# Block-diagonal gates of a recurrent head group as 64-row products on the two halves of the array

## The chip, the cores and the metric

The kernel runs on one core of one Trainium2 chip. The metric is the device time of one execution in microseconds (us), as the median of several runs. The engines are named as in the profile: PE is TensorE (PEld are its weight loads), DVE is VectorE, ACT is ScalarE, POOL is GpSimd, and SP is the engine that issues the DMAs.

## The reference

One layer of a hybrid trunk, on a prompt of 2048 positions of width 1024 and on 8 short sequences of 4 positions (the decode part). A pre-norm and a modulation give hn; one projection gives six groups of 512 columns; group A (RG-LRU) and group B (HGRN2) run side by side; one output projection, a post-norm and a gated residual follow. What the change touches are the two gates r and i of group A, whose weights are eight diagonal blocks of 64 x 64 each:

```python
def _rglru(x, h0, wa, ba, wx, bx, lam):
    B, L, _ = x.shape
    xb = x.reshape(B, L, N_BLK_A, BLK_A)
    r = jax.nn.sigmoid(jnp.einsum('blnc,ncd->blnd', xb, wa).reshape(B, L, D_A) + ba)
    i = jax.nn.sigmoid(jnp.einsum('blnc,ncd->blnd', xb, wx).reshape(B, L, D_A) + bx)
    log_a = -C_RGLRU * jax.nn.softplus(-lam.astype(jnp.float32)) * r.astype(jnp.float32)
    a = jnp.exp(log_a)
    u = jnp.sqrt(jnp.maximum(-jnp.expm1(2.0 * log_a), 0.0)) * (i * x).astype(jnp.float32)
    u = u.at[:, 0].add(a[:, 0] * h0.astype(jnp.float32))
    _, h = lax.associative_scan(_lin_comb, (a, u), axis=1)
    return h, h[:, -1]
```

## The kernel before

The prompt is worked through in 8 bodies of 256 positions (body 0, a loop over bodies 1 to 6, body 7); the decode part is the tail behind body 7. Each engine has its own program, written out by hand in one order, and semaphores tie them together. `Signal.at(n, j)` is the count that a semaphore has reached after j steps of body n. An engine that waits holds up everything behind it on its queue.

Within a body the four blocks of 128 channels of group A, and the four heads of group B, are taken in two halves, p = 0 and p = 1. TensorE's order in a body is: projections of the forget gate and q for p = 0 (`project`, L390, three products of 16-bit halves for each fp32 one); between them `turn_y` of the body before (L441); row projections of v and the gate path with the levels of group B (`level`, L462, L464, L469) in between; the output rows of the body before (`out_rows`, L390); `turn_k` (L477) and the two units (`unit`, L491 to L493); then the same for p = 1, with xa and ga of group A. The first gates, `gates(n, 0)`, stand behind level 3 of p = 1, ahead of the second half of a projection. The second gates, `gates(n, 1)`, stand behind `turn_k(n, 1)` and six products of `out_rows`, ahead of the two units that end the body. The next body begins with a wait for `i_sig` (the sigmoids of i), then `project` twice (48 products), then `turn_y`, which waits for `yb_ok` (the scaled rows that VectorE writes, L1195) and writes the banks aux.

`gates` (L507) makes four fp32 products of 128 x 128 weights with 256 columns: two blocks for r into one bank of aux, two for i into the other, each tied to its own semaphore (gr_ps, gi_ps). Half of every weight tile in `wg` is zero, since the blocks are 64 wide; POOL zeroes it at the start. Levels 1 to 5 use 64 columns of q; level 6 (L469) uses column tiles of 32, level 7 of 64. In the tail, `d_states` (L757) has products of 32 rows, and the decode gates (L794) are eight products with 32 columns.

ScalarE's order around the first gates is `ga_out`, `gates_out` (two sigmoids for r, L903, two for i, L908, each 128 x 256 with a bias per partition), `xa_out` (L879), `decay`, `root`. Around the second gates it is `k_out` (the copy that kt_sb counts, L865), `squares_m` (L861), `gates_out`, `squares_o` of one unit (L872), `squares_m`, `squares_o` of the other unit, `decay`, `root`. VectorE's `rows` waits for the last squares, takes a reciprocal root in twelve small steps and scales four blocks (L1195). POOL's `gated` multiplies i by the convolved input.

At the start SP issues the loads of the conditioning, two early weight pieces, ten rows of parameters (L307, into `am`, turned by TensorE into `par`, from which `pcol` takes the biases), and then the weight pieces in order, with `wg` behind piece 6.

Of the kernel before, what the change touches and what calls it, by code (L numbers as in the profile page):

```python
# [38 lines left out]
ACT = mybir.ActivationFunctionType  # L39
# [28 lines left out]
_at = 0  # L68
for _name, _n in (("pre", KT), ("post", KT), ("cw", CW * CT), ("cb", CT), ("ba", CT), ("bx", CT), ("lam", CT),
                  ("lbl", CT), ("onw", CT), ("adab", 3 * KT)):  # L70
    ROW[_name] = _at
    _at += _n
# [3 lines left out]
def build(nc, x_prompt, x_sample, state_rglru_h, state_rglru_conv, state_hgrn_S, c_prompt, c_sample, ada_w, ada_b,  # L76
          pre_norm_w, post_norm_w, w_in, conv_w, conv_b, rg_wa, rg_ba, rg_wx, rg_bx, rg_lambda, hg_lb_logits,
          hg_onorm_w, w_out, y_prompt, y_sample, h_prompt, conv_prompt, S_prompt, h_sample, conv_sample, S_sample):
    with ExitStack() as ctx:
# [33 lines left out]
        sil = sb("sil", [P, CT, T])  # L113
        wg = sb("wg", [P, 2, CT, P])

# [57 lines left out]
        u_ps = Signal("u_ps", 4)  # L173
        gr_ps, gi_ps = Signal("gr_ps", 2), Signal("gi_ps", 2)

# [4 lines left out]
        xa_sb, ga_sil = Signal("xa_sb", 2), Signal("ga_sil", 2)  # L180
        r_sig, i_sig, a_exp, th_ok = (Signal(s, 4) for s in ("r_sig", "i_sig", "a_exp", "th_ok"))
        u_sqrt = Signal("u_sqrt", 2)
# [109 lines left out]
        def _(sp):  # L292
# [12 lines left out]
            for name, src in loads:  # L305
                rows = src.rearrange("(r c) -> r c", c=P)
                sp.dma_start(am[ROW[name]:ROW[name] + rows.shape[0], 0, :], rows).then_inc(par_ld, 16)  # L307
            for i, (kind, c) in enumerate(pieces):
                if i == 3:
                    for t in range(NT):  # L310
                        sp.dma_start(xin[:, t, :], xp_rows[t]).then_inc(xld[t].sem, 16)
                if i == 13:
                    for t in range(NT):
                        load_x(1, t)
                if before[kind, c]:
                    pk, pc = before[kind, c]
# [12 lines left out]

# [51 lines left out]
        def _(pe):  # L381
# [50 lines left out]
            def turn_y(n, j):  # L432

                if j == 0:
                    pe.wait_ge(yb_ok.sem, yb_ok.at(n, 8))
                    pe.wait_ge(r_sig.sem, r_sig.at(n, 4))
                else:
                    pe.wait_ge(i_sig.sem, i_sig.at(n, 4))
# [57 lines left out]
            def gates(n, p):  # L496
                pe.wait_ge(cvc.sem, cvc.at(n, 8 * p + 8))
                for w, s in ((0, gr_ps), (1, gi_ps)):
                    if p == 0 and w == 0:
                        if not isinstance(n, int) or n > 0:  # L500
                            pe.wait_ge(ytl.sem, ytl.at(n - 1, 2))
                    elif w == 1:
                        pe.wait_ge(kt_sb.sem, kt_sb.at(n, p + 1))
                    elif not (isinstance(n, int) and n == BODIES - 1):
                        pe.wait_ge(hn_lo.sem, hn_lo.at(n + 1, 2))
                    for c in range(2):
                        last = mm(aux[(1 + w + p) % 2][:, T * c:T * c + T], wg[:, w, 2 * p + c, :], xc[:, c, :],  # L507
                                  start=True, stop=True)
                    last.then_inc(s.sem, 1)

# [35 lines left out]
            def body(n, first, last_body):  # L546
# [7 lines left out]
                if not first:  # L554
                    pe.wait_ge(i_sig.sem, i_sig.at(n - 1, 4))
                project(ring[0], FR, 0, n)
# [108 lines left out]
                level(n, 1, 6)  # L665
                pe.wait_ge(r_sig.sem, r_sig.at(n, 2))
                if not last_body:
                    turn_x(n + 1, 0)
                    pe.wait_ge(i_sig.sem, i_sig.at(n, 2))
                    turn_x(n + 1, 1)  # L670
                    pe.wait_ge(yb_ok.sem, yb_ok.at(n, 4))
                    pe.wait_ge(s_upd.sem, s_upd.at(n, 4))
                    turn_x(n + 1, 2)
                    turn_x(n + 1, 3)
                else:
                    pe.wait_ge(i_sig.sem, i_sig.at(n, 2))
                    turn_decode()
# [33 lines left out]
            for i in range(NEARLY):  # L711
                if i == 2:
                    pe.wait_ge(par_ld, 160)
# [7 lines left out]
            pe.wait_ge(wg_ld, 64)  # L721
            pe.wait_ge(zeroed, 3)
            pe.wait_ge(carry_zero, 2)
# [37 lines left out]
            pe.wait_ge(dv("hn"), 1)  # L761
            pe.wait_ge(i_sig.sem, i_sig.at(n - 1, 4))
            for i, col in enumerate([b + P * c for b in (XA, GA, Q_, FR) for c in range(CT)]):
# [79 lines left out]
        def _(act):  # L843
# [66 lines left out]
            def decay(n, p):  # L910

                act.wait_ge(r_sig.sem, r_sig.at(n, 2 * p + 2))
                for c in range(2):
# [163 lines left out]
            act.wait_ge(dv("gates_ps"), 1)  # L1077
            for w, dst, bias in ((0, rrd, "ba"), (1, iid, "bx")):
                for c in range(CT):
                    o = W4 * w + TD * c  # L1080
                    A(dst[:, TD * c:TD * c + TD], lev[1][:, o:o + TD], ACT.Sigmoid, bias=pcol(bias, c)).then_inc(dv("ri_d"), 1)
            act.wait_ge(dv("ri_d"), 2 * CT)
            for c in range(CT):
# [27 lines left out]
        def _(dve):  # L1111
# [325 lines left out]
            rest(2)  # L1437
            dve.wait_ge(zeroed, 3)

# [76 lines left out]
            dve.wait_ge(dv("a_d"), 2 * CT)  # L1516
            dve.wait_ge(dv("ri_d"), 2 * CT)
            link(V.tensor_tensor(iid, iid, xcd, ALU.mult))
# [53 lines left out]
        def _(pool):  # L1572
# [31 lines left out]
            def gated(n, p):  # L1604

                pool.wait_ge(i_sig.sem, i_sig.at(n, 2 * p + 2))
# [45 lines left out]
            def link(ins):  # L1652
# [75 lines left out]
```

## Time and profile before

| | |
|---|---|
| median of 3 runs | 1025.59 us (1025.47 to 1027.35) |
| profiled execution: span, its own time | 1026.3 us |
| PE busy | 984.2 us, 96% |
| PEld busy | 714.3 us, 70% |
| DVE busy | 582.0 us, 57% |
| ACT busy | 430.0 us, 42% |
| POOL busy | 161.0 us, 16% |
| gates on PE (L507) | 128 passes in 16 calls |

How to read it: the profile is one execution. A busy PE is not PE at its peak, since its products are pipelined and their ends are modelled; starts are the safer number. The chain follows the work that ended last back to what released each step. In a timeline, instructions of one kind that follow each other are one row with their count, and in brackets stands how long the engine was idle before and for whom.

### The profile page before, as it was taken

The page shows a single profiled execution, that of the slowest core. Times are in us where ns is not written, and L with a number is a line of the kernel's source. Part 1 is how long each engine was busy: PE and PEld are TensorE (multiplying, and loading weights), DVE is VectorE, ACT ScalarE, POOL GpSimd, SP SyncE. Part 2 cuts the span into 40 slices and gives each one's busy share as a digit, 9 for nine tenths or more (in the row PEclk, how much of TensorE's full clock was granted, in tenths as well). Part 3 has the DMA queues.
Part 4 walks back from the last instruction along what each step waited for, and adds up shares of the span by engine and source line. Part 5 has one row for each costly group of instructions (what it writes and reads, how often), then busy time and mean ns, then how long its engine had stood idle before and what let it go on. Part 6 is the DMA issues. An engine that isn't in the chain of part 4 may idle for free.

```text
span 1026.3 us, 19994 instructions
## 1 busy us (share of the span) xinstructions
PE 984.2 (96%) x7423; PEld 714.3 (70%) x7478; DVE 582.0 (57%) x1652; ACT 430.0 (42%) x810; POOL 161.0 (16%) x208
## 2 busy tenths in 40 slices
PE   7899986899999999999999999999999999999987
PEld 3465875469775887579766976697759775887554
DVE  1453688436763576436754566366635773477445
ACT  2531747313651365135713373237413661345321
POOL 4000024301130112011110112011301130111212
PEclk9999998899999999999999999999999999999998
DMA  9984301100110011000110011001101010100413
GB/s 313 326 275 130 118 24 59 62 2 21 42 63 0 20 41 43 19 20 0 42 62 0 21 41 62 0 21 41 62 0 41 0 50 1 42 1 23 118 42 111
DMA packets 46590, 60.62 MB, mean 59 GB/s; under 512 B 2748, under 2 KB 40208, under 8 KB 46524
## 3 DMA queue, kind: packets, MB, share of 16 engines
q1 hardware_dynamic: 46524, 59.86, 17.8%
q8 instruction: 27, 0.44, 0.2%
q14 instruction: 39, 0.32, 0.1%
HBM read 48.90 MB, written 10.95 MB: 58 GB/s over the span
## 4 chain that ended last, share of the span: by engine, by line
PE 90%; DVE 5%; issue 2%; ACT 1%; DMA 1%; SPq 1%; DVEq 0%; ACTq 0%
PE ring L390 66%; PE lev L464 7%; PE aux L507 3%; PE okv L521 2%; PE lev L469 1%; PE okv L491 1%; PE lev L462 1%; PE ring L521 1%; PE okv L493 1%; PE okv L492 1%; DMA work<-in_w_in_dram 1%; PE okv L811 1%; PE aux L441 1%; PE aux L477 1%; PE aux L428 1%
## 5 line engine op out<-in xcount | busy, mean ns | idle before, releaser
L390 PE MATMUL ring<-hnh,wih 128*128 128x256 bf16 (+1 forms) x1152 | 291.1, 264 | 5.8 <-DVE hnl L1273 4.2
L390 PE MATMUL ring<-hnh,wil 128*128 128x256 bf16 (+1 forms) x1152 | 291.2, 264 | 0.0
L390 PE MATMUL ring<-hnl,wih 128*128 128x256 f16 (+1 forms) x1152 | 291.1, 264 | 0.0
L390 PE MATMUL ring<-woh,work 128*128 128x512 f16 x512 | 162.3, 379 | 1.7
L390 PEld LDWEIGHTS ring<-hnh,wih 128*128 128x128 f16 x1152 | 112.5, 100 | 18.1 <-issue 4.5
L1165 DVE TENSOR_TENSOR qq<-qq,gg 128x256 f32<-128x256 f32 x96 | 44.1, 459 | 140.1 <-PE lev L464 99.8
L390 PEld LDWEIGHTS ring<-hnl,wih 128*128 128x128 f16 x1152 | 110.6, 98 | 12.9
L390 PEld LDWEIGHTS ring<-hnh,wil 128*128 128x128 bf16 x1152 | 110.6, 98 | 12.4
L390 PE MATMUL ring<-wih,hnh 128*128 128x512 f16 (+1 forms) x264 | 101.1, 383 | 4.0 <-ACT kk L851 4.0
L390 PE MATMUL ring<-wih,hnl 128*128 128x512 f16 (+1 forms) x264 | 101.1, 383 | 1.4 <-issue 0.2
L1587 POOL TENSOR_TENSOR kk<-kk,cols 128x256 f32<-128x256 f32 x32 | 29.3, 935 | 419.3 <-ACT kk L851 419.3
L390 PE MATMUL ring<-wil,hnh 128*128 128x512 bf16 (+1 forms) x240 | 91.7, 382 | 0.0
L390 PEld LDWEIGHTS ring<-woh,work 128*128 128x128 bf16 (+1 forms) x512 | 50.2, 98 | 54.8
L464 PEld LDWEIGHTS lev<-qq,kk 128*128 128x128 f32 x640 | 80.9, 192 | 8.5 <-issue 2.3
L390 PE MATMUL ring<-wol,work 128*128 128x512 bf16 x225 | 85.3, 379 | 0.0
L464 PE MATMUL lev<-qq,kk 128*128 128x64 f32 x640 | 80.4, 268 | 1.8 <-DVE kk L1166 1.7
L1183 DVE SCALAR_TENSOR_TENSOR st<-st,gg,okv 128x128 f32<-128x128 f32 x64 | 19.4, 345 | 70.9 <-PE okv L493 70.9
L1173 DVE COPY_PREDICATED am<-lmask,lev 128x256 f32<-128x256 uint8 (+1 forms) x112 | 57.3, 511 | 0.0
L861 ACT ACTIVATE ring<-ring 128x512 f32<-128x512 f32 x32 | 18.6, 582 | 84.0 <-DVE work L1204 84.0
L1607 POOL TENSOR_TENSOR ii<-ii,xc 128x512 f32<-128x512 f32 x16 | 22.9, 1429 | 188.3 <-ACT ii L908 188.2
L390 PEld LDWEIGHTS ring<-wih,hnh 128*128 128x128 bf16 (+1 forms) x264 | 28.2, 107 | 29.6 <-ACT kk L851 4.3
L390 PEld LDWEIGHTS ring<-wih,hnl 128*128 128x128 f16 (+1 forms) x264 | 26.0, 99 | 31.8 <-issue 1.1
(310 smaller groups left out, 1585.5 us busy)
## 6 DMA issues: line engine op xcount, KB each, us to landing
xin<-in_x_prompt_dram SPq DMA_DIRECT2D x16, 512.0 KB, 3.4
work<-in_x_prompt_dram SPq DMA_DIRECT2D x16, 512.0 KB, 4.3
out_dram<-work SPq DMA_DIRECT2D x16, 512.0 KB, 2.6
work<-in_ada_w_dram SPq DMA_DIRECT2D x4, 1024.0 KB, 10.4
woh<-in_ada_w_dram SPq DMA_DIRECT2D x4, 1024.0 KB, 11.8
work<-in_w_in_dram SPq DMA_DIRECT2D x4, 1024.0 KB, 7.2
woh<-in_w_in_dram SPq DMA_DIRECT2D x4, 1024.0 KB, 8.5
wol<-in_w_in_dram SPq DMA_DIRECT2D x4, 1024.0 KB, 9.6
```

The source lines that it names most:

```text
L390: last = mm(out, a(k), b(k), start=start and k == ks[0] and j == 0, stop=stop and k == ks[-1] and j == 2)
L428: last = nc.tensor.transpose(bank[:, (k % 2) * T + P * t:(k % 2) * T + P * t + P], xin[:, t, P * k:P * k + P], ident[:, :])
L441: last = nc.tensor.transpose(aux[j][:, T * h + P * t:T * h + P * t + P], gbs[:, t, P * (2 * j + h):P * (2 * j + h) + P], ident[:, :])
L464: last = mm(lev[i % 2][:, P // 2 * hc:P // 2 * hc + P // 2], k, blocks(q, m)[:, :, 1, :], start=True, stop=True)
L507: last = mm(aux[(1 + w + p) % 2][:, T * c:T * c + T], wg[:, w, 2 * p + c, :], xc[:, c, :], start=True, stop=True)
L521: last = mm(bank[0:NS, o:o + 256], siluc[:, k, :], w[:, k, :], start=k == 0, stop=k == KT - 1)
L861: A(ring[j % 2][:, :], ring[j % 2][:, :], ACT.Square, accum_out=essq[:, j:j + 1]).then_inc(esq[j % 2].sem, 1)
L1165: V.tensor_tensor(qo, qo, g[:, :, 0:1].to_broadcast([P, nb, m]), ALU.mult).then_inc(q_upd.sem, 1)
L1173: V.copy_predicated(a[:, :, :, 1, :], msk, x).then_inc(amask.sem, 1)
L1183: V.scalar_tensor_tensor(st[:, hd, :], st[:, hd, :], gg[:, o:o + 1], okv[c][:, 2 * P + P * h:3 * P + P * h], ALU.mult, ALU.add).then_inc(s ...
L1587: G.tensor_tensor(kk[:, cols], kk[:, cols], omlb[:, hd:hd + 1].to_broadcast([P, T]), ALU.mult)\
L1607: G.tensor_tensor(ii[:, :, :], ii[:, :, :], xc[:, :, :], ALU.mult).then_inc(ix_ok.sem, 1)
```

## The change

One weight tile `wg[:, c, :]` of 128 x 128 now holds both gates of two blocks. Its upper 64 rows hold r in columns 0 to 63 and i in columns 64 to 127; its lower 64 rows hold i in columns 0 to 63 and r in columns 64 to 127. A product takes 64 rows of weights and of the input, and writes 128 rows: r and i of one block. Products of the upper rows write aux[0], those of the lower rows aux[1]. So r stands on the partitions of its channels, and i on the other half of the partitions; its sigmoid reads one half and writes the other, with a bias that is loaded with its halves exchanged (`bxs`, two further DMAs). There are four sigmoids for r and four for i in each call, of 64 rows each. One semaphore (g_ps) stands for all four products, and the waits for both banks come ahead of them. The decode gates are done in the same way, into lev[1] and aux[0], with 16 sigmoids in place of 8. The zeroing of `wg` and the wait for it fall away. The core of the diff:

```diff
-        wg = sb("wg", [P, 2, CT, P])
+        wg = sb("wg", [P, CT, P])
...
+            rows = rg_bx[0].rearrange("(r c) -> r c", c=P)
+            for half in range(2):
+                sp.dma_start(am[ROW["bxs"]:ROW["bxs"] + CT, 0, 64 * half:64 * half + 64],
+                             rows[:, 64 - 64 * half:128 - 64 * half]).then_inc(par_ld, 16)
...
-                    sp.wait_ge(zeroed, 1)
                     for w, src in ((0, rg_wa), (1, rg_wx)):
                         for odd in range(2):
                             v = src[0].rearrange("(t two) c d -> two c t d", two=2)[odd]
-                            sp.dma_start(wg[64 * odd:64 * odd + 64, w, :, 64 * odd:64 * odd + 64], v).then_inc(wg_ld, 16)
+                            o = 64 * (odd ^ w)
+                            sp.dma_start(wg[64 * odd:64 * odd + 64, :, o:o + 64], v).then_inc(wg_ld, 16)
...
             def gates(n, p):
                 pe.wait_ge(cvc.sem, cvc.at(n, 8 * p + 8))
-                for w, s in ((0, gr_ps), (1, gi_ps)):
-                    if p == 0 and w == 0:
-                        if not isinstance(n, int) or n > 0:
-                            pe.wait_ge(ytl.sem, ytl.at(n - 1, 2))
-                    elif w == 1:
-                        pe.wait_ge(kt_sb.sem, kt_sb.at(n, p + 1))
-                    elif not (isinstance(n, int) and n == BODIES - 1):
-                        pe.wait_ge(hn_lo.sem, hn_lo.at(n + 1, 2))
-                    for c in range(2):
-                        last = mm(aux[(1 + w + p) % 2][:, T * c:T * c + T], wg[:, w, 2 * p + c, :], xc[:, c, :],
-                                  start=True, stop=True)
-                    last.then_inc(s.sem, 1)
+
+                if p == 0:
+                    if not isinstance(n, int) or n > 0:
+                        pe.wait_ge(ytl.sem, ytl.at(n - 1, 2))
+                elif not (isinstance(n, int) and n == BODIES - 1):
+                    pe.wait_ge(hn_lo.sem, hn_lo.at(n + 1, 2))
+                pe.wait_ge(kt_sb.sem, kt_sb.at(n, p + 1))
+                for c in range(2):
+                    for odd in range(2):
+                        rows = slice(64 * odd, 64 * odd + 64)
+                        last = mm(aux[odd][:, T * c:T * c + T], wg[rows, 2 * p + c, :], xc[rows, c, :], start=True, stop=True)
+                last.then_inc(g_ps.sem, 1)
...
-                pe.wait_ge(r_sig.sem, r_sig.at(n, 2))
+                pe.wait_ge(i_sig.sem, i_sig.at(n, 4))
                 if not last_body:
                     turn_x(n + 1, 0)
-                    pe.wait_ge(i_sig.sem, i_sig.at(n, 2))
                     turn_x(n + 1, 1)
...
-            for w in range(2):
-                for c in range(CT):
-                    o = TD * CT * w + TD * c
-                    last = mm(lev[1][:, o:o + TD], wg[:, w, c, :], xcd[:, TD * c:TD * c + TD], start=True, stop=True)
+            for c in range(CT):
+                for odd, bank in ((0, lev[1]), (1, aux[0])):
+                    rows = slice(64 * odd, 64 * odd + 64)
+                    last = mm(bank[:, TD * c:TD * c + TD], wg[rows, c, :], xcd[rows, TD * c:TD * c + TD], start=True, stop=True)
...
-                act.wait_ge(gr_ps.sem, gr_ps.at(n, p + 1))
+                act.wait_ge(g_ps.sem, g_ps.at(n, p + 1))
                 act.wait_ge(iu.sem, iu.at(n, p))
                 for c in range(2):
-                    A(rr[:, c, :], aux[(1 + p) % 2][:, T * c:T * c + T], ACT.Sigmoid,
-                      bias=pcol("ba", 2 * p + c)).then_inc(r_sig.sem, 1)
-                act.wait_ge(gi_ps.sem, gi_ps.at(n, p + 1))
+                    for odd in range(2):
+                        rows = slice(64 * odd, 64 * odd + 64)
+                        A(rr[rows, c, :], aux[odd][rows, T * c:T * c + T], ACT.Sigmoid,
+                          bias=pcol("ba", 2 * p + c)[rows, :]).then_inc(r_sig.sem, 1)
                 act.wait_ge(scan.sem, scan.at(n, 2 * p))
                 for c in range(2):
-                    A(ii[:, c, :], aux[p][:, T * c:T * c + T], ACT.Sigmoid, bias=pcol("bx", 2 * p + c)).then_inc(i_sig.sem, 1)
+                    for odd in range(2):
+                        rows, src = slice(64 * odd, 64 * odd + 64), slice(64 - 64 * odd, 128 - 64 * odd)
+                        A(ii[rows, c, :], aux[odd][src, T * c:T * c + T], ACT.Sigmoid,
+                          bias=pcol("bxs", 2 * p + c)[src, :]).then_inc(i_sig.sem, 1)
...
-            G.memset(wg[:, :, :, :], 0.0).then_inc(zeroed, 1)
```

Everything else follows from this: r_sig and i_sig count 8 in a body instead of 4, so waits on them count twice as far, and ri_d counts 16.

## Rows read from the trace of the kernel before

**Rows 1.** The page: busy time of the engines, and the chain by engine.

```profile
PE 984.2 (96%) x7423; PEld 714.3 (70%) x7478; DVE 582.0 (57%) x1652; ACT 430.0 (42%) x810; POOL 161.0 (16%) x208
PE 90%; DVE 5%; issue 2%; ACT 1%; DMA 1%; SPq 1%; DVEq 0%; ACTq 0%
```

**Rows 2.** A stretch: its length, busy of PE, PEld, DVE, ACT, POOL, PEclk, DMA share, GB/s.

```profile
446.55:554.98 108.43, 108.06 (x811) 80.75 (x817) 61.98 (x184) 46.66 (x93) 15.22 (x19) 1.00 0.08 29
```

**Rows 3.** The chain in the body from 446.55: start, us, what.

```profile
473.54 1.78 PE aux L507 x8
497.35 1.73 PE aux L507 x8
```

**Rows 4.** TensorE's timeline, level 6: start, us, what, count.

```profile
484.79 0.45 PE L469 MATMUL lev<-qq,kk 128*32 128x32 f32 x16
```

**Rows 5.** TensorE's timeline in the tail, products of 32 rows.

```profile
1006.29 0.38 PE L390 MATMUL ring<-woh,wil 128*32 128x512 f16 x1
1006.61 1.15 PE L757 MATMUL lev<-vv,ktr 32*128 32x128 f32 x8
1007.60 1.05 PE L757 MATMUL okv<-gbs,ktr 32*128 32x128 f32 x8
1008.58 0.39 PE L390 MATMUL ring<-woh,wil 128*32 128x512 f16 x1
```

**Rows 6.** ScalarE's timeline at the first gates.

```profile
474.50 0.84 ACT L903 ACTIVATE rr<-aux,par 128x256 f32<-128x256 f32 x2 [3.32 <-PE aux L507]
...
478.12 0.60 ACT L879 ACTIVATE xa<-ring 128x512 f32<-128x512 f32 x1 [1.92 <-PE ring L390]
```

**Rows 7.** ScalarE's timeline at the second gates.

```profile
496.09 0.60 ACT L865 ACTIVATE ktr<-aux 128x512 f32<-128x512 f32 x1 [2.76 <-PE aux L477]
497.60 0.58 ACT L861 ACTIVATE ring<-ring 128x512 f32<-128x512 f32 x1 [0.91 <-DVE work L1204]
...
498.30 1.28 ACT L903 ACT_TABLE_LOAD   x1
499.60 0.84 ACT L903 ACTIVATE rr<-aux,par 128x256 f32<-128x256 f32 x2
500.33 0.84 ACT L908 ACTIVATE ii<-aux,par 128x256 f32<-128x256 f32 x2
...
502.53 0.58 ACT L861 ACTIVATE ring<-ring 128x512 f32<-128x512 f32 x1 [0.52 <-DVE work L1204]
...
503.81 0.28 ACT L872 ACTIVATE junk<-okv 128x128 bf16<-128x128 f32 x1 [0.59 <-DVE st L1183]
```

**Rows 8.** VectorE's timeline behind them.

```profile
504.61 0.17 DVE L1125 TENSOR_SCALAR stat<-stat 128x4 f32<-128x4 f32 x1 [0.83 <-ACT junk L872]
...
506.99 1.13 DVE L1195 SCALAR_TENSOR_TENSOR gbs<-okv,stat,gbs 128x128 f32<-128x128 f32 x4
```

**Rows 9.** TensorE's timeline at the start of the next body.

```profile
502.88 0.27 PE L390 MATMUL ring<-hnh,wih 128*128 128x256 bf16 x1
...
508.01 0.27 PE L390 MATMUL ring<-hnh,wil 128*128 128x256 bf16 x1
508.18 0.33 PE L441 MATMUL aux<-ident,gbs 128*128 128x128 f32 x1
```

**Rows 10.** The stretch of body 0's second half, columns as in rows 2.

```profile
130.00:187.00 57.00, 41.42 (x322) 35.22 (x321) 47.32 (x92) 36.36 (x56) 21.61 (x11) 0.86 0.12 38
```

**Rows 11.** TensorE's and ScalarE's timelines in the tail.

```profile
970.34 1.97 PE L794 MATMUL lev<-xin,wg 128*128 128x32 f32 x16
972.14 0.38 PE L390 MATMUL ring<-woh,work 128*128 128x512 f16 x1
...
991.92 0.27 ACT L1097 ACTIVATE junk<-okv 32x128 bf16<-32x128 f32 x1 [5.62 <-PE okv L811]
```

**Rows 12.** SP's timeline at the start: DMA issues.

```profile
5.31 0.29 SPq L307 DMA_DIRECT2D am<-in_rg_bx_dram  x1
5.64 0.29 SPq L307 DMA_DIRECT2D am<-in_rg_lambda_dram  x1
```

More of the change, by code:

```diff
@@ L68 @@
 _at = 0
-for _name, _n in (("pre", KT), ("post", KT), ("cw", CW * CT), ("cb", CT), ("ba", CT), ("bx", CT), ("lam", CT),
+for _name, _n in (("pre", KT), ("post", KT), ("cw", CW * CT), ("cb", CT), ("ba", CT), ("bx", CT), ("bxs", CT), ("lam", CT),
                   ("lbl", CT), ("onw", CT), ("adab", 3 * KT)):
@@ L173, in build @@
         u_ps = Signal("u_ps", 4)
-        gr_ps, gi_ps = Signal("gr_ps", 2), Signal("gi_ps", 2)
+        g_ps = Signal("g_ps", 2)
         f_sig, k_sig, q_sb = Signal("f_sig", 2), Signal("k_sig", 2), Signal("q_sb", 2)
@@ L180, in build @@
         xa_sb, ga_sil = Signal("xa_sb", 2), Signal("ga_sil", 2)
-        r_sig, i_sig, a_exp, th_ok = (Signal(s, 4) for s in ("r_sig", "i_sig", "a_exp", "th_ok"))
+        r_sig, i_sig = Signal("r_sig", 8), Signal("i_sig", 8)
+        a_exp, th_ok = Signal("a_exp", 4), Signal("th_ok", 4)
         u_sqrt = Signal("u_sqrt", 2)
@@ L435, in turn_y @@
                     pe.wait_ge(yb_ok.sem, yb_ok.at(n, 8))
-                    pe.wait_ge(r_sig.sem, r_sig.at(n, 4))
-                else:
-                    pe.wait_ge(i_sig.sem, i_sig.at(n, 4))
+                    pe.wait_ge(i_sig.sem, i_sig.at(n, 8))
                 for h in range(2):
@@ L554, in body @@
                 if not first:
-                    pe.wait_ge(i_sig.sem, i_sig.at(n - 1, 4))
+                    pe.wait_ge(i_sig.sem, i_sig.at(n - 1, 8))
                 project(ring[0], FR, 0, n)
@@ L675, in body @@
                 else:
-                    pe.wait_ge(i_sig.sem, i_sig.at(n, 2))
                     turn_decode()
@@ L712, in _ @@
                 if i == 2:
-                    pe.wait_ge(par_ld, 160)
+                    pe.wait_ge(par_ld, 192)
                     nc.tensor.transpose(aux[0][:, 0:NROW], am[0:NROW, 0, :], ident[0:NROW, 0:NROW]).then_inc(pre_ps, 1)
@@ L721, in _ @@
             pe.wait_ge(wg_ld, 64)
-            pe.wait_ge(zeroed, 3)
+            pe.wait_ge(zeroed, 2)
             pe.wait_ge(carry_zero, 2)
@@ L761, in _ @@
             pe.wait_ge(dv("hn"), 1)
-            pe.wait_ge(i_sig.sem, i_sig.at(n - 1, 4))
+            pe.wait_ge(i_sig.sem, i_sig.at(n - 1, 8))
             for i, col in enumerate([b + P * c for b in (XA, GA, Q_, FR) for c in range(CT)]):
@@ L898, in gates_out @@
             def gates_out(n, p):
-                act.wait_ge(gr_ps.sem, gr_ps.at(n, p + 1))
+                act.wait_ge(g_ps.sem, g_ps.at(n, p + 1))
                 act.wait_ge(iu.sem, iu.at(n, p))
                 for c in range(2):
-                    A(rr[:, c, :], aux[(1 + p) % 2][:, T * c:T * c + T], ACT.Sigmoid,
-                      bias=pcol("ba", 2 * p + c)).then_inc(r_sig.sem, 1)
-                act.wait_ge(gi_ps.sem, gi_ps.at(n, p + 1))
+                    for odd in range(2):
+                        rows = slice(64 * odd, 64 * odd + 64)
+                        A(rr[rows, c, :], aux[odd][rows, T * c:T * c + T], ACT.Sigmoid,
+                          bias=pcol("ba", 2 * p + c)[rows, :]).then_inc(r_sig.sem, 1)
                 act.wait_ge(scan.sem, scan.at(n, 2 * p))
                 for c in range(2):
-                    A(ii[:, c, :], aux[p][:, T * c:T * c + T], ACT.Sigmoid, bias=pcol("bx", 2 * p + c)).then_inc(i_sig.sem, 1)
+                    for odd in range(2):
+                        rows, src = slice(64 * odd, 64 * odd + 64), slice(64 - 64 * odd, 128 - 64 * odd)
+                        A(ii[rows, c, :], aux[odd][src, T * c:T * c + T], ACT.Sigmoid,
+                          bias=pcol("bxs", 2 * p + c)[src, :]).then_inc(i_sig.sem, 1)
             def decay(n, p):
-                act.wait_ge(r_sig.sem, r_sig.at(n, 2 * p + 2))
+                act.wait_ge(r_sig.sem, r_sig.at(n, 4 * p + 4))
                 for c in range(2):
@@ L1077, in _ @@
             act.wait_ge(dv("gates_ps"), 1)
-            for w, dst, bias in ((0, rrd, "ba"), (1, iid, "bx")):
+            for dst, bias, w in ((rrd, "ba", 0), (iid, "bxs", 1)):
                 for c in range(CT):
-                    o = W4 * w + TD * c
-                    A(dst[:, TD * c:TD * c + TD], lev[1][:, o:o + TD], ACT.Sigmoid, bias=pcol(bias, c)).then_inc(dv("ri_d"), 1)
-            act.wait_ge(dv("ri_d"), 2 * CT)
+                    for odd, bank in ((0, lev[1]), (1, aux[0])):
+                        rows, src = slice(64 * odd, 64 * odd + 64), slice(64 * (odd ^ w), 64 * (odd ^ w) + 64)
+                        A(dst[rows, TD * c:TD * c + TD], bank[src, TD * c:TD * c + TD], ACT.Sigmoid,
+                          bias=pcol(bias, c)[src, :]).then_inc(dv("ri_d"), 1)
+            act.wait_ge(dv("ri_d"), 4 * CT)
             for c in range(CT):
@@ L1437, in _ @@
             rest(2)
-            dve.wait_ge(zeroed, 3)
+            dve.wait_ge(zeroed, 2)
             body(0, True, False)
@@ L1516, in _ @@
             dve.wait_ge(dv("a_d"), 2 * CT)
-            dve.wait_ge(dv("ri_d"), 2 * CT)
+            dve.wait_ge(dv("ri_d"), 4 * CT)
             link(V.tensor_tensor(iid, iid, xcd, ALU.mult))
@@ L1604, in gated @@
             def gated(n, p):
-                pool.wait_ge(i_sig.sem, i_sig.at(n, 2 * p + 2))
+                pool.wait_ge(i_sig.sem, i_sig.at(n, 4 * p + 4))
                 G.tensor_tensor(ii[:, :, :], ii[:, :, :], xc[:, :, :], ALU.mult).then_inc(ix_ok.sem, 1)
```

## Prediction

> **What bounds the kernel now.** I read the page first: TensorE is busy for 96% of the span, and the chain of work that ended last runs through it for 90% [rows 1]. So a microsecond taken from TensorE's queue can shorten the run, and one added to ScalarE (42% busy) costs nothing unless TensorE comes to wait for it. The table of stretches then shows where this holds: from the middle of body 1 to the middle of body 7 lie six stretches of a body's length that are alike, of 108.4 us each, of which TensorE is busy for 108.06 at the full granted clock, so no slack is left [rows 2]. The chain inside one body shows the two places that the change touches: the first gates (gates(n, 0)) hold TensorE for 1.78 us and the second gates (gates(n, 1)) for 1.73, eight passes each, since each of the four fp32 products is recorded as two passes of 0.216 us [rows 3].
>
> **What the change does to a gates block.** Each call still has four products and eight passes, but a product now uses one half of the rows of the array, and neighbours in the queue use different halves and write different banks. No row here has two row halves at work. The nearest are the column tiles of level 6: 16 passes of 32 columns start within 0.25 us (0.45 less the last one's 0.20) [rows 4]. One behind another they would need 16 x 0.027 = 0.43 (0.216 x 32 / 256). So they ran two at a time. By that, eight passes need four steps: 4 x 0.216 = 0.86 us.
>
> Going into and out of a tiled shape costs something. The products of 32 rows in the tail show it [rows 5]: the product before starts at 1006.29 and takes 0.22, the first tiled one comes at 1006.61 (0.10 late); its second weight load is not hidden, since eight passes take 0.99 there where 8 x 0.111 = 0.89 is the pace (0.10); after the last one, due to end at 1008.49, the next shape starts at 1008.58 (0.09). Together 0.29, say 0.30. So a block takes 0.30 + 0.86 = **1.16 us**, 0.62 less than the first gates and 0.57 less than the second. From the other side, all eight passes in a row give 0.30 + 1.73 = 2.03, 0.25 more than now.
>
> **First gates, seven bodies.** TensorE goes on at once with project and level 4. ScalarE has eight sigmoids instead of four; a 64-row sigmoid I take to cost what a 128-row one costs, because the length along a row is the same. They follow one another every 0.365 us (499.60 to 500.33 for two [rows 7]), so four more cost 1.46. They start at about 474.64 (now 474.50 [rows 6]) and end at 477.56. The next thing on ScalarE, xa_out, waits for TensorE until 478.12 now, after 1.92 us of idle time [rows 6], and would be due 0.62 earlier, at 477.50: 0.06 late. The moved wait of TensorE (all of i_sig ahead of turn_x, past 485) has over 7 us to spare, and kt_sb of the first half is long there. So the full 0.62 counts: 7 x 0.62 = **4.3 us gained** in bodies 1 to 7.
>
> **Second gates.** The wait on kt_sb now stands ahead of all four products, with the units queued behind it; the copy that it waits for ends at 496.69 [rows 7] and the gates start at 497.19: no cost. But ScalarE is next. It comes free at 498.30, loads its table until 499.58 without waiting for the gates (ahead of the first gates it sat idle for 3.32 us with the load behind it [rows 6]), and starts the sigmoids at 499.60 [rows 7]; the new block would be ready at about 498.45, so that start stays. Eight sigmoids then end their turn at 499.60 + 8 x 0.365 = 502.52. Behind them come, in order, squares_o of one unit (0.80, as from 503.81 to the release of VectorE at 504.61 [rows 7, 8]), squares_m (0.70, as from 497.60 to 498.30 [rows 7]) and squares_o of the last unit (0.80): 504.82. Now this is 504.61, because ScalarE has two gaps there, behind TensorE's units and products (0.52 and 0.59 us of idle time [rows 7]). From there VectorE needs 3.5 us to the last scaled row at 508.12 [rows 8], and turn_y of the next body starts at 508.18, while TensorE's projection ends at 508.12 [rows 9]. So turn_y is already released at the last moment, and comes at 508.39: **0.21 later** than now, although TensorE itself would be ready earlier (it waits for i_sig at the start of the body until 502.69, then projects for 5.24, until 507.93). The gain of the second gates is lost, and 0.21 more, in the six bodies that have such a successor: 6 x 0.21 = 1.3 us. The ends of this term: if the squares were not held up at all, a gain of 0.57 a body; if sigmoids didn't overlap and took their full 0.47, 8 x 0.47 + 2.30 ends at 505.66, 1.05 lost a body. I take 0.21, since the spacing is read from the same instruction. In body 7 the tail projects for 9.65 us before turn_y, so only the wait for i_sig counts: 0.2 gained.
>
> **Body 0.** From 130 to 187 us TensorE is busy for 41 of 57 us and waits for VectorE, ScalarE and the weight preparation [rows 10]. I count 0, with 1.5 to either side, for the eight sigmoids more stand in that ScalarE queue too.
>
> **Tail.** The decode gates are 16 passes of 0.112 us, bound by weight loads, in 1.80 us [rows 11]. In pairs: 8 x 0.112 + 0.15 = 1.05, so 0.75 gained; one by one 0.1 lost. ScalarE's eight further sigmoids (at most 8 x 0.47 = 3.8) lie ahead of 5.62 us in which it is idle until TensorE's next result [rows 11].
>
> **Start.** Two more DMAs on SP's queue stand ahead of all weight loads. An issue takes 0.34 there (5.31 to 5.64 [rows 12]), so the bound is 0.68 us later; none, if the transfers are the bound. These are 8 short rows against the 80 long ones of the parameters already there, so I take 0.2. The memset of wg that falls away had no one waiting.
>
> **Sum.** -4.3 + 1.3 - 0.2 - 0.75 + 0.2 = -3.75 us. The profiled execution's own time is its span, 1026.3; the median of the runs is 1025.59, 0.07% below, so I subtract from that: **1021.9 us**.
>
> **Rivals.**
> *Five steps instead of four.* In the program the two passes of one product stand next to each other: top, top, bottom, bottom. If passes start strictly in that order, a second pass waits for the first of its own half, and only neighbours of different halves overlap: five steps, 1.38 us a block. First gates gain 0.40, the tail 0.65, the rest as above: -2.8 + 1.3 - 0.2 - 0.65 + 0.2 = -2.15, 1023.4 us. The 0.25 us of the column tiles [rows 4] leave eight or nine steps open. The Trainium skill states such an order (TensorE: Matmul & The Clock Gate, Part 3, The mechanism): matmuls of different tiles overlap, but start and end in the order of the program. No run here shows it for row tiles; by that rule the sum would be this rival's.
>
> *Slower: the halves take turns.* Eight passes in a row make a block of 2.03 us: 7 x 0.25 in the first gates, 0.30 x 6 in the second (there turn_y moves with TensorE's units), 0.3 in body 7, 0.1 in the tail, 0.2 at the start: +4.2, 1029.8 us. Since the switch costs 0.30, the change pays only if fewer than about 6.5 of 8 steps are left. Rows 4 speak against it, but for column tiles only.
>
> *The second gates' gain is kept.* If something shortens ScalarE's queue between 499.60 and 504.61 (cheaper sigmoids on half the rows), each body gives 0.57 more: about 1017.
>
> *ScalarE costs more.* Sigmoids that read one half of the partitions and write the other, or a late start of the weights, cost 2 us more: about 1024.5.
>
> **How the numbers follow.** Forecast 0.55, five steps 0.15, halves in turn 0.12, gain kept 0.10, dearer ScalarE 0.08. The range reaches from the gain kept to the dearer ScalarE with body 0 and the start at their ends, 1017 to 1026.5; it leaves out the halves in turn and the far side of the gain kept. A difference of 0.2% (2.05 us) is about what a measurement can tell from no change. Below 1023.5 lie nearly all of the forecast (0.51), the gain kept (0.10) and half of the five steps (0.07): faster 0.67. Slower than 1027.6 is the rival of turns: 0.12. The rest, 0.21, is the same.
>
> **What would show it.** In the profile after: the chain's first gates at about 1.2 us (1.4 for five steps, 2.0 in turn); ScalarE's squares following the sigmoids without a gap from 499.6 on (in the body's own time); a wait of some 0.4 us ahead of turn_y for VectorE's gbs, and a body of about 108.0 us. The prediction is wrong if a body is not 0.3 to 0.5 shorter, above all if turn_y shows no wait or a wait over 1 us.

## The result and the profile after

The changed kernel is slower: 1030.22 us (median of 13 runs) against 1025.95 us for the kernel before (13 runs), a ratio of 1.0035 (95% interval 1.0026 to 1.0045). The forecast was 1021.9 us with a range up to 1026.5, so both the sign and the range were wrong. The profiled execution has a span of 1030.6 us, 4.3 us above the one before. Executions of one kernel spread with the mean granted TensorE clock (19 of the kernel before: 1023.80 us at 0.987, 1027.24 to 1029.12 us at 0.981), so the profiles are compared part by part.

The page of the kernel after, busy times and the chain by engine (compare [rows 1]):

```profile
PE 981.7 (95%) x7478; PEld 702.0 (68%) x7478; DVE 591.0 (57%) x1652; ACT 465.6 (45%) x882; POOL 159.7 (15%) x207
PE 77%; DVE 11%; ACT 6%; issue 4%; DMA 1%; SPq 1%; POOL 0%; DVEq 0%; ACTq 0%; POOLq 0%
```

TensorE has less to do, and its share of the chain falls from 90% to 77%: VectorE and ScalarE now hold 11 points more of it, and issue 2. The timeline of TensorE around the first gates of one body:

```profile
477.28 0.39 PE L467 MATMUL lev<-qq,kk 128*128 128x64 f32 x2
477.60 1.13 PE L511 MATMUL aux<-xc,wg 64*128 64x256 f32 x8
478.66 0.28 PE L395 MATMUL ring<-hnh,wih 128*128 128x256 bf16 x1
```

From the first pass to the next product are 1.06 us, where eight passes one behind another took 1.78 [rows 3]. So the halves do work side by side, in four steps. That is also visible in the tail, where neighbours write different banks and so stand in rows of their own; each pair starts within 0.01 us:

```profile
976.00 0.29 PE L795 MATMUL lev<-xin,wg 64*128 64x32 f32 x1
976.00 0.29 PE L795 MATMUL aux<-xin,wg 64*128 64x32 f32 x1
976.13 0.27 PE L795 MATMUL lev<-xin,wg 64*128 64x32 f32 x1
976.13 0.27 PE L795 MATMUL aux<-xin,wg 64*128 64x32 f32 x1
```

What went wrong stands on ScalarE, at the second gates (answers to [rows 7, 8]):

```profile
501.81 1.28 ACT L906 ACT_TABLE_LOAD   x1
503.11 1.95 ACT L906 ACTIVATE rr<-aux,par 64x256 f32<-64x256 f32 x4
505.09 1.96 ACT L912 ACTIVATE ii<-aux,par 64x256 f32<-64x256 f32 x4
507.07 0.28 ACT L873 ACTIVATE junk<-okv 128x128 bf16<-128x128 f32 x1
```

Four 64-row sigmoids take 1.98 us to the next, 0.495 each; eight take 3.96 us. In the kernel before, 128-row ones follow every 0.365 us [rows 7]. TensorE then waits twice (answers to [rows 9]): at the start of the body for i, and at turn_y, which starts 0.27 us after the projection is through (512.31 and its step of 0.11):

```profile
507.17 0.28 PE L395 MATMUL ring<-hnh,wih 128*128 128x256 bf16 x1 [1.08 <-ACT ii L912]
512.31 0.27 PE L395 MATMUL ring<-hnh,wil 128*128 128x256 bf16 x1
...
512.69 1.09 PE L444 MATMUL aux<-ident,gbs 128*128 128x128 f32 x8
```

Five bodies from one level 0 to the same one, before and after (the columns are those of [rows 2]; the level before starts at 245.24, so a body is 542.16 / 5 = 108.43 us before, and 544.12 / 5 = 108.82 us after):

```profile
245.20:787.40 542.20, 540.35 (x4047) 403.78 (x4081) 313.70 (x920) 233.32 (x455) 75.73 (x95) 1.00 0.08 30
```

```profile
248.58:792.70 544.12, 538.21 (x4083) 395.44 (x4082) 318.71 (x920) 253.60 (x495) 75.34 (x95) 1.00 0.08 30
```

TensorE is busy 0.43 us less in a body and ScalarE 4.06 us more. Where the 4.3 us of the span come from, by the starts of the same instructions in the two traces: 0.3 at the start, 3.1 in body 0, 0.39 in each of bodies 1 to 6 (2.35 in all), nothing in body 7, and 1.3 gained in the tail.

### The profile page after: what moved, and what is told of

The parts are those of the page before. It is cut to its first block, busy times and chain, and to the rows that moved or that the text cites. A ratio compares the mean times of both kernels' runs of the same rounds, so it can differ in the third digit from the quotient of the medians.

```text
span 1030.6 us, 20113 instructions
## 1 busy us (share of the span) xinstructions
PE 981.7 (95%) x7478; PEld 702.0 (68%) x7478; DVE 591.0 (57%) x1652; ACT 465.6 (45%) x882; POOL 159.7 (15%) x207
## 4 chain that ended last, share of the span: by engine, by line
PE 77%; DVE 11%; ACT 6%; issue 4%; DMA 1%; SPq 1%; POOL 0%; DVEq 0%; ACTq 0%; POOLq 0%
PE ring L395 57%; PE lev L467 6%; DVE xc L1240 2%; PE okv L524 2%; PE lev L465 1%; PE lev L472 1%; PE ring L524 1%; DVE hnl L1280 1%; ACT ii L912 1%; ACT rr L906 1%; PE aux L511 1%; PE okv L494 1%; DMA work<-in_w_in_dram 1%; ACT L906 1%; PE okv L496 1%
## 5 line engine op out<-in xcount | busy, mean ns | idle before, releaser
L395 PE MATMUL ring<-wil,hnh 128*128 128x512 bf16 (+1 forms) x264 | 101.3, 384 | 0.0
L395 PE MATMUL ring<-wol,work 128*128 128x512 bf16 x256 | 97.0, 379 | 0.0
L1614 POOL TENSOR_TENSOR ii<-ii,xc 128x512 f32<-128x512 f32 x16 | 20.7, 1295 | 226.4 <-ACT ii L912 226.4
L979 ACT ACTIVATE gbs<-ring 128x512 f32<-128x512 f32 x16 | 9.6, 598 | 89.7 <-PE ring L395 89.7
```

Of the source, the lines that this page charges most:

```text
L395: last = mm(out, a(k), b(k), start=start and k == ks[0] and j == 0, stop=stop and k == ks[-1] and j == 2)
```

## The experiments

The theory was that the eight sigmoids cost the time because they lost their overlap. The rivals put it on TensorE's side (its moved waits), on the exchange of halves, or on any 64-row sigmoid. "Body" below is the mean of five bodies, as in the two rows above. Ratios are against the kernel before, with 95% intervals; it was measured again beside the runs, at 1026.58 us for the first four below, 1027.06 for the next four and 1026.10 for the last three.

**The order of the sigmoids.**

```diff
-  r: for c: for odd;  then  i: for c: for odd
+  for odd:  r of c = 0, 1;  then i of c = 0, 1
```

> The changed kernel with its eight sigmoids of a gates call in another order: first all that read bank aux[0] (r of both blocks, then i of both blocks), then all that read aux[1]. So of seven pairs of neighbours four read the same half of the partitions, the same bank, and write the same half; two change only the half that is read; one changes bank and written half. In the changed kernel every neighbour changes the bank and the written half, and all follow at 0.495 us. Theory (a change of half or bank keeps two sigmoids from overlapping): 0.365 us in the four like pairs, so the eight take about 3.42 us instead of 3.94; turn_y is released some 0.5 us earlier in each body and the time falls by about 4 us, to 1026. Rival (a 64-row sigmoid costs 0.495 us whatever its neighbour is): every pair stays at 0.495 us and the time at about 1030.

Measured: 1024.71 us, ratio 0.9983 (0.9971 to 0.9995), body 108.28. ScalarE's timeline:

```profile
497.94 0.83 ACT L907 ACTIVATE rr<-aux,par 64x256 f32<-64x256 f32 x2
498.79 0.83 ACT L910 ACTIVATE ii<-aux,par 64x256 f32<-64x256 f32 x2
499.65 0.83 ACT L907 ACTIVATE rr<-aux,par 64x256 f32<-64x256 f32 x2
500.50 0.83 ACT L910 ACTIVATE ii<-aux,par 64x256 f32<-64x256 f32 x2
501.36 0.28 ACT L873 ACTIVATE junk<-okv 128x128 bf16<-128x128 f32 x1
```

Eight take 3.42 us (497.94 to 501.36), as the theory had it. Within a pair the second starts 0.37 us after the first (0.83 less one duration of 0.46); from pair to pair it is 0.48. That is no partial overlap: the second of a pair lasts 0.457 us instead of 0.469, and the next one starts 0.025 us behind its end, just as in the kernel after. The step from r to i keeps the bank and the written half and changes the half that is read; the step in the middle changes bank and written half and reads the same half. Either one ends the overlap. A change of bank or of the written tile doesn't do it: 128-row r and i have other banks and other tiles and follow at 0.36 us [rows 7]. With this order alone the change is no loss.

**TensorE's part alone.**

```diff
-  A(rr[rows, c], aux[odd][rows, ...]) x4;  A(ii[rows, c], aux[odd][src, ...]) x4
+  A(rr[:, c], aux[0][:, ...]) x2;  A(ii[:, c], aux[1][:, ...]) x2
```

> TensorE's part alone: the products of the changed kernel, but ScalarE takes the two banks as they lie with four sigmoids of 128 rows, as in the kernel before (it leaves out the exchange of halves, so i and half of r are not those of the reference; the tail is as changed). Theory (the loss is ScalarE's four further sigmoids): both gates keep TensorE's gain, 0.61 and about 0.57 us a body, so a body takes about 107.25 us against 108.83 of the changed kernel, body 0 comes back to about that of the kernel before, and the time is about 1017. Rival (the loss is on TensorE's side: waits for both banks placed ahead of all four products, the moved i_sig wait): a body stays at 108.4 or above and the time above 1024.

Measured: 1019.12 us, ratio 0.9929 (0.9910 to 0.9949):

```profile
246.19:782.97 536.78, 534.93 (x4047) 395.43 (x4081) 312.08 (x920) 231.81 (x455) 74.29 (x95) 1.00 0.08 31
```

A body takes 107.36 us, 1.07 less than before and 1.46 less than after. Products, waits and loads are those of the change; so the loss is in the sigmoids, and TensorE's side of the forecast was sound.

**ScalarE's part alone.**

```diff
-  A(rr[:, c, :], aux[(1 + p) % 2][:, ...])
+  for odd: A(rr[rows, c, :], aux[(1 + p) % 2][rows, ...])      (and so for ii)
```

> ScalarE's part alone: the kernel before with its dense 128-row products, but every sigmoid of the gates split in two of 64 rows (read and written half the same). Theory (further sigmoids at 0.495 us, without overlap, are the cost): eight end 1.9 us later than the four, turn_y of the next body is about 1.05 us later in each of the six bodies that have one, body 0 loses some 3 us, and the time is about 1034.5. Rival (a 64-row sigmoid follows at 0.365 us here too, or what costs is the exchange of halves): 0.2 us a body, about 1027.

Measured: 1034.56 us, ratio 1.0080 (1.0060 to 1.0100):

```profile
245.51:793.33 547.82, 541.74 (x4047) 403.70 (x4081) 313.88 (x920) 254.15 (x495) 74.46 (x95) 1.00 0.08 30
```

A body takes 109.56 us, 1.13 more than before. ScalarE's timeline:

```profile
502.13 1.95 ACT L906 ACTIVATE rr<-aux,par 64x256 f32<-64x256 f32 x4
504.11 1.95 ACT L913 ACTIVATE ii<-aux,par 64x256 f32<-64x256 f32 x4
506.09 0.28 ACT L873 ACTIVATE junk<-okv 128x128 bf16<-128x128 f32 x1
```

The four r sigmoids start from 502.13 to 503.62, every 0.495 us, though none exchanges halves and all four read one bank. So the exchange is not what costs. The 3 us expected in body 0 did not come: only 0.5 (below).

**i behind the squares.**

```diff
   r_out(n, 1); squares_o(n, 2); squares_m(n - 1, 3); squares_o(n, 3)
+  i_out(n, 1)
...
-  pe.wait_ge(i_sig, 8 of body n - 1)   ahead of the first project
+  pe.wait_ge(r_sig, 8 of body n - 1)
```

> The changed kernel with the four i sigmoids of the second gates moved behind the last squares on ScalarE; the wait of TensorE at the start of a body is then for r_sig (which stands behind the squares that free its ring bank), and the wait for i_sig stays where it is needed, at turn_y. Theory (what is lost is the place of the eight sigmoids ahead of the squares and of the next body's projection): the squares end about as early as TensorE's units allow, TensorE starts the body without its wait of 1.1 us, both gains count, a body takes about 107.3 us and the time is about 1019 to 1020.5. Rival (later work of ScalarE, decay, root and the gates of the next body, comes later by the same amount and TensorE waits for that instead): a body stays at 108.4 or above, the time at 1026 or above.

Measured: 1026.63 us, ratio 0.9997 (0.9984 to 1.0010), body 108.32. The squares did end early and the wait at the start of the body is gone, but turn_y was late by 0.9 us. VectorE and POOL at that place:

```profile
508.44 0.16 DVE L1141 SCALAR_TENSOR_TENSOR stat<-stat 128x4 f32<-128x4 f32 x1
508.64 1.12 DVE L1142 SCALAR_TENSOR_TENSOR stat<-stat 128x4 f32<-128x4 f32 x1
```

```profile
508.47 1.27 POOL L1618 TENSOR_TENSOR ii<-ii,xc 128x512 f32<-128x512 f32 x1 [16.56 <-ACT ii L914]
```

A step of four elements a row takes 1.12 us instead of 0.16, and ends with POOL's product, which the late i moved there.

**POOL behind the small steps.**

```diff
+  if p: pool.wait_ge(newt_u, all steps of body n)
   G.tensor_tensor(ii, ii, xc, ALU.mult)
```

> The kernel with the late i sigmoids (run e4_late_i), and one wait more: POOL's product of i and the convolved input in the second half waits until VectorE's twelve small steps are done. In e4_late_i this POOL product (1.27 us, from 508.47) and the last small step of VectorE (1.12 us instead of 0.16, from 508.64 to 509.76) end together. Theory (the two exclude each other, and VectorE lost 0.96 us to POOL there): the last step takes 0.16 us again, turn_y is about 0.85 us earlier in each body, a body takes about 107.45 us instead of 108.31 and the time is about 1021.5. Rival (the step is long for another reason, or POOL's later product makes root and the next body's gates late by as much): a body stays at 108.0 or above and the time at 1025 or above.

Measured: 1026.95 us, ratio 1.0006 (0.9990 to 1.0022), body 108.32. The collision is gone:

```profile
508.65 0.17 DVE L1142 SCALAR_TENSOR_TENSOR stat<-stat 128x4 f32<-128x4 f32 x1
508.85 1.13 DVE L1206 SCALAR_TENSOR_TENSOR gbs<-okv,stat,gbs 128x128 f32<-128x128 f32 x4
```

That half of the theory holds: turn_y comes 0.95 us earlier than in the run before. The time stays, and TensorE's waits in the next stretch (510 to 620) show what took the place of the one at turn_y (lev is a level of group B, in us, times, longest):

```profile
PE lev L467 <- DVE qq L1160: 0.7, 1, 0.7
```

ScalarE works in a ring: sigmoids, squares, decay, root, the gate of the next body, from which VectorE makes q and k for the levels. Taken from ahead of the squares, the longer sigmoids delay the other end of the same ring. In this profile the late sigmoids run until 508.43 and root until 513.6; POOL's first product of the next body then waits for ScalarE until 516.08, and VectorE's qq ends at 525.60, ahead of the level that waits (525.75). The Trainium skill (SBUF — State Buffer, Who interferes with whom) says that a VectorE instruction with two inputs in SBUF and a GpSimd instruction that reads there exclude each other for a whole instruction. The 1.12 us that become 0.17 here agree.

**New products in the first gates alone.**

```diff
+  dense = lambda n, p: p == 1      (dense tiles, four sigmoids for the second gates)
```

> The changed kernel with the new products and eight sigmoids in the first gates and the tail alone; the second gates of every body are dense 128-row products with four sigmoids again (further weight tiles, two further weight loads at the start). Theory (the first gates' gain of 0.61 us a body is whole, the loss is all in the second gates and in body 0): a body takes 107.8 us, 0.61 below the kernel before, bodies 1 to 7 give 4.3 us and the tail about 1.2; body 0 may take back up to 1.5 us; the time is about 1021 to 1022. Rival (the eight sigmoids of the first gates also delay something that TensorE needs): a body at 108.2 or above, the time at 1024 or above.

Measured: 1025.10 us, ratio 0.9986 (0.9975 to 0.9998):

```profile
248.24:787.35 539.11, 537.26 (x4047) 400.07 (x4081) 318.88 (x920) 242.67 (x475) 75.43 (x95) 1.00 0.08 31
```

A body takes 107.82, exactly the 0.61 us less that the theory had. The total misses it by 3 to 4 us; part of that is the higher base of these runs. In the profiled execution 2.8 us are lost in body 0 and 1.9 more ahead of it, of which 1.7 are back before the half of body 0. Those 1.7 go with the clock: of all 13 traces, nine (that of the kernel before too) have 3.4 us at a granted clock of 0.50 there, near 110 us, and take 60.7 us from the first level 0 to the second; four (this one too) have none and take 59.05.

**Four quarters.**

```diff
-  mm(aux[odd][:, ...], wg[rows, 2 * p + c, :], xc[rows, c, :])
+  for w: mm(aux[w][to, ...], wg[rows, 2 * p + c, to], xc[rows, c, :])     (to: half odd ^ w)
-  eight sigmoids of 64 rows
+  r: two of 128 rows;  i: four of 64 rows, by halves
```

> The changed kernel with each product cut into two of 64 columns of weights, so that four quarters of the array are used: r of both halves goes to aux[0] on the partitions of its channels, i to aux[1] on the other half. r then takes two sigmoids of 128 rows, i four of 64 rows, in the order that keeps neighbours on one half. 16 passes instead of eight, and one small product of 8 columns ahead of them. Theory A (four quarters run at the same time): passes start four by four in four steps, a block takes about 1.3 us, the six sigmoids 2.45 us, a body about 107.6 us, the time about 1021. Theory B (two at a time): eight steps, a block of about 2.1 us, a body of 108.9 us or more, the time at 1030 or above.

Measured: 1025.89 us, ratio 0.9996 (0.9985 to 1.0007), body 108.20. TensorE at the first gates:

```profile
473.71 0.38 PE L508 MATMUL aux<-xc,wg 64*128 64x8 f32 x2
474.03 1.09 PE L513 MATMUL aux<-xc,wg 64*64 64x256 f32 x16
475.05 0.28 PE L395 MATMUL ring<-hnh,wih 128*128 128x256 bf16 x1
```

Sixteen passes take 1.02 us: four at a time, in four steps. On TensorE theory A holds, but its time doesn't: the small product ahead of them costs 0.32 us in each call.

**All three together.** Late i, POOL behind the small steps, and sigmoids by halves:

> As e5_late_i_pool, and both kinds of sigmoids in the order of e1_sig_order within themselves (the two of one half next to each other, in both gates). Theory: each four take 1.71 us instead of 1.95; in bodies 1 to 6 the squares then wait for TensorE's units and VectorE, so turn_y hardly moves and a body takes 107.3 to 107.45 us; body 0, where the eight sigmoids stand on the path, gives 1 to 2 us; the time is about 1019.5 to 1021. Rival (the order is worth its 0.24 us in every body): a body at 107.2 or below, the time below 1019.

Measured: 1024.92 us, ratio 0.9981 (0.9969 to 0.9994), body 108.10. Against the run with POOL behind the small steps a body gains 0.22 us. Both the r and the late i sigmoids are 0.24 shorter in each call, so a part of what is taken out of the ring counts in every body; which part, no run isolates. Both body times expected were too low, since they were worked out without the ring: TensorE still waits 0.6 us at the same level of group B.

**Four quarters without the small product.**

```diff
-  gates_wait(n, p); mm(aux[0][:, 0:8], ...); 16 products
+  gates_wait(n, p) ahead of level 3 (p = 0), ahead of the last out_rows product (p = 1); 16 products
```

> The quarters of run e7_quadrants (four at a time, four steps) without the small product of 8 columns ahead of them: the waits of the gates stand in front of earlier products instead (level 3 for the first gates, the last of the out_rows products for the second). In e7_quadrants the small product holds TensorE for 0.32 us in each call (473.71 to 474.03), and the second gates' sigmoids started 0.4 us later than in the kernel before's place, at 499.99 against 499.60, so a body took 108.20 us. Theory (each call gives its 0.3 us back, and the six sigmoids of 2.55 us end early enough for squares, rows and turn_y): a body takes about 107.6 us, the time is about 1021.5 to 1022.5. Rival (ScalarE's ring of sigmoids, squares, decay, root and the next body's gates holds a body at 108.0 or above, as in e5_late_i_pool): the time at 1024 or above.

Measured: **1021.68 us, ratio 0.9954 (0.9938 to 0.9971)**. This beats both kernels.

```profile
472.80 1.09 PE L516 MATMUL aux<-xc,wg 64*64 64x256 f32 x16
473.83 0.28 PE L397 MATMUL ring<-hnh,wih 128*128 128x256 bf16 x1
```

```profile
498.45 0.84 ACT L912 ACTIVATE rr<-aux,par 128x256 f32<-128x256 f32 x2
499.31 1.68 ACT L918 ACTIVATE ii<-aux,par 64x256 f32<-64x256 f32 x4
501.02 0.28 ACT L881 ACTIVATE junk<-okv 128x128 bf16<-128x128 f32 x1
```

```profile
246.30:784.13 537.83, 535.44 (x4127) 393.70 (x4161) 318.42 (x920) 240.86 (x475) 75.51 (x95) 1.00 0.08 31
```

The block is as short as that of the change, the sigmoids take 2.57 us instead of 3.96, and a body takes 107.57 us, as expected.

**The moved wait alone.**

```diff
+  pe.wait_ge(kt_sb, ...)               ahead of all four products of the kernel before
-  elif w == 1: pe.wait_ge(kt_sb, ...)
```

> The kernel before with one thing of the change: the wait for kt_sb ahead of all four products of a gates call, instead of ahead of the two that write its bank. Theory (it costs nothing in bodies 1 to 7, where the copy ends 0.5 us before the gates, but in body 0 the products then start behind the copy, at about +5.4 us from turn_k instead of +4.4): second gates of body 0 about 1.0 us later, body 1 about 0.5 to 1.0 later, bodies 2 to 6 at 108.43 as before; time +0.5 to +1.0. Rival (body 0's loss comes from the sigmoids alone): body 0 unchanged, no difference in time.

Measured: 1027.75 us, ratio 1.0016 (1.0006 to 1.0027). In the profile the second gates of body 0 start 5.38 us behind turn_k instead of 4.39, as the theory had it, but level 0 of body 1 comes no later (193.93 against 194.13), and a body takes 108.43. So the profiled execution shows the delay and no price for it. The 1.7 us of the timed runs have no place in it, but the comparison can't settle them: the profiled execution of the kernel before has a span of 1026.3 us, 1.9 above that of its median run (1024.4). That stays open.

**The moved wait undone in body 0.**

```diff
+  if n == 0 and p: r products; g0_ps; wait kt_sb; i products
```

> Run e10_quads_free, and in body 0 alone the second gates take r first (two of four quarters at a time), then wait for kt_sb, then i, with a semaphore of r's own, so that the r sigmoids start as early as in the kernel before. Theory (the moved wait is worth 1.0 us in body 0): 1.0 us below e10_quads_free. Rival (other waits of body 0 take its place): the same time as e10_quads_free within 0.3 us.

Measured: 1021.57 us, ratio 0.9948 (0.9934 to 0.9961). The gates of body 0 start 1.04 us earlier against turn_k, and level 0 of body 1 only 0.4; in the time the two can't be told apart. The rival holds.

## Why the prediction was wrong

**The block on TensorE: right.** 1.16 us was forecast; 477.60 to 478.66 and some 0.1 of entry are that. The first gates give 0.61 us a body against 0.62, here and in the run with the first gates alone. Halves in turn and five steps both fall. The Trainium skill (TensorE: Matmul & The Clock Gate, Part 3, The mechanism) says that matmuls start and end in the order of the program, the rule behind the rival of five steps. For starts that holds here for products and not for the two passes of one: the pairs of the tail alternate between the two banks, so a second pass starts behind the first pass of the next product.

**The sigmoids of the second gates: the step that failed.** "I take 0.21, since the spacing is read from the same instruction." It wasn't the same: the row has 128 rows and no change of half. The term was 8 x 0.365 = 2.92 and measured 3.96. The other end, without overlap, was worked out at 1.05 lost a body; the second gates lost 1.00 (0.39 more a body in spite of 0.61 gained). That is 0.79 x 6 = 4.7 us of the 8.1 by which the span misses the sum; body 0 is 3.1 more. The run with the order by halves, where overlap returns, and the run with dense products and split sigmoids, where it goes, show the cause from both sides. The Trainium skill (ScalarE: Activation LUTs, What ACT_TABLE_LOAD costs) gives 280 + 0.833 x 256 = 493 ns for such an instruction and 93 ns of overlap between neighbours, so 0.40 us from start to start, as an estimate. The 0.495 us agree with that price without overlap; with overlap 0.365 to 0.37 us were measured.

**Body 0: mis-sized.** Counted as 0 with 1.5 to either side; in the profiles it lost 3.15 us from level 0 of its second half to level 0 of body 1 (70.83 to 73.98). With the same products and four sigmoids it is 71.73, so the split sigmoids carry 2.25 of it. Without the moved wait they cost little there (71.35 with dense products), and the moved wait alone costs nothing (70.42). Of the 3.15, 1.08 stand ahead of turn_k (35.30 us from level 0 before, 36.38 after), as many as with dense products and split sigmoids (36.37), so they come from the first gates' sigmoids. For the rest the traces suggest a reason that no run isolates: in the kernel before ScalarE idles 1.16 us behind the second gates' sigmoids, until VectorE's fold of a weight piece has ended (at 168.71); the late start (the moved wait) and the longer turn each fit into that, and both don't.

TensorE's granted clock differs there as well. It stood at 0.50 (1.2 GHz) for 10.2 us before and for 20.5 us after:

```profile
157.50:167.70 10.20, 5.78 (x18) 4.72 (x19) 10.09 (x17) 9.28 (x16) 4.07 (x1) 0.50 0.00 0
```

```profile
154.50:175.00 20.50, 10.98 (x50) 9.07 (x51) 16.31 (x29) 18.48 (x33) 6.20 (x4) 0.50 0.31 103
```

It fell while TensorE waited for VectorE (4.00 us of idle time until 158.61 before, 3.57 until 155.16 after). The run with four sigmoids has the low clock for as long (153.9 to 174.4), so the 2.25 us are not the clock's; how much of the other 0.9 is, stays open.

**Body 7, tail, start.** Body 7 was to give 0.2 beside its first gates; its second gates lost 0.5, again by the sigmoids. The decode gates gave 0.79 (forecast 0.75) up to turning the last rows, and 0.5 more came behind them, up to the next products of 32 rows (9.19 us before, 8.67 after); the granted clock was 0.64 there before and 0.68 after, which no run isolates as the cause. The start was 0.29 later (forecast 0.2) in the trace of after, and -0.07 to 0.98 in the other runs with just these two loads, so it says little.

**What was right beside a wrong sum.** TensorE did come to wait for ScalarE's queue, at the two waits named. Of the signs of being wrong, the body's length told (0.39 longer instead of 0.3 to 0.5 shorter), and turn_y did not: it waited 0.27 us, where 0.4 was forecast, because most of the wait moved to the start of the body (1.08 us), as the last i sigmoid ended only at 507.04. "Gain kept" turned out to need fewer sigmoids, not only cheaper ones. Two small slips change nothing: 1025.59 less 3.75 is 1021.84, and the 1026.3 of the trace is a span, which in the timed runs is 1.7 us or more shorter than the time, so it is not to be set beside the median time of 1025.59.

## What to carry to other kernels

Splitting a product over halves of the array splits what reads it as well: count the instructions behind it at a spacing measured for that shape and that order of halves, not for a full tile. Where halves must be read apart, put neighbours on the same half; better, choose the quarters so that one output lies whole. And when an engine off the chain (42% busy) stands in a ring with the one that sets the pace, moving its work to another place in the ring gives back little: here 0.50 of the 1.46 us that a body had lost against four sigmoids, and the 0.95 us then won at one wait gave nothing. Taking work out of the ring did more (107.57 us a body with six sigmoids, 107.36 with four).

## What the runs showed of the hardware

Two sigmoids of 64 rows and 256 columns overlapped by 0.09 to 0.1 us only where they read and write the same halves: 0.37 us from start to start. Where the read half, the written half or both change, the next starts 0.025 us behind the end of the one before. That makes 0.48 us behind the second of an overlapping pair and 0.495 behind one that did not overlap; whether one half changes or both makes no difference (both change in the middle of the i sigmoids of the four quarters, at 0.48; only the written one between r and i in the kernel after, at 0.495). At 32 columns the same loss shows: 0.31 us from start to start in the tail of the kernel after, where 128-row ones follow every 0.17 us in the kernel before.

Four quarters of the array ran at the same time. The timeline of the run without the small product, cut to 0.04 us (472.79 to 472.83), has the first four passes in it:

```profile
472.80 0.45 PE L516 MATMUL aux<-xc,wg 64*64 64x256 f32 x4
```

Four passes of 64 x 64 weights in each quarter took the four steps that four passes in each half had taken.

A step of VectorE on 128 x 4 elements took 1.12 us instead of 0.16 next to a GpSimd product, and 0.17 when that product was put behind it.
